# Expert rows loaded into all 128 partitions, the last weight chunks held, and three expert places of 32 tokens, in a hybrid SSD/GLA/MoE decoder step

## What is computed

```python
h2 = (rms_norm(x, p['norm2_w']) * (1 + sc2) + sh2).reshape(bt * s, D_MODEL)
comb = route(h2, w_router, router_bias)          # two experts of one group per token, weights sum to 1
for e in range(N_EXPERTS):
    ye = (jax.nn.silu(h @ wg[e]) * (h @ wu[e])) @ wd[e]
    out = out + comb[:, e:e + 1].astype(h.dtype) * ye
x = x + g2 * y_moe
```

## Time and profile before

| what | us |
|---|---|
| median of 3 runs | 1023.16 (1021.93 to 1028.83) |
| the profiled execution | 1020.22 |
| its span, first to last instruction | 1018.3 |

### The profile page before, as it was taken

The page is one execution under the profiler, slowest core; times in us unless marked ns, Lnnn a source line. Parts: engine busy times, 40 slices in busy tenths (PEclk is TensorE's granted clock), DMA queues, the critical chain, the costliest instruction groups (busy, mean ns, idle before and its releaser), DMA issues.

```text
span 1018.3 us, 18707 instructions
## 1 busy us (share of the span) xinstructions
PE 941.1 (92%) x7658; PEld 654.9 (64%) x7658; DVE 443.6 (44%) x1110; ACT 225.4 (22%) x459; POOL 151.4 (15%) x238
## 2 busy tenths in 40 slices
PE   5999999999999999999999999998999889889653
PEld 3667676676767566666666677665887658755331
DVE  3121234677347975666540711226534232232216
ACT  2240222323353322332251300003200011011012
POOL 0000232352021543233200000011100000000022
PEclk9999999999999999999999999999999989889996
DMA  9943345465455566546442633442899999999992
GB/s 375 393 151 124 125 165 189 168 232 176 170 189 206 206 221 212 207 168 238 164 150 88 254 122 125 188 184 89 291 354 388 374 382 383 364 390 375 364 383 79
DMA packets 47323, 239.43 MB, mean 235 GB/s; under 512 B 6896, under 2 KB 10576, under 8 KB 23920
## 3 DMA queue, kind: packets, MB, share of 16 engines
q1 hardware_dynamic: 42560, 227.74, 60.4%
q0 software_dynamic: 1552, 5.51, 1.6%
q10 hardware_dynamic: 3120, 4.92, 1.5%
HBM read 214.70 MB, written 23.83 MB: 234 GB/s over the span
## 4 chain that ended last, share of the span: by engine, by line
PE 73%; DMA 13%; SPq 6%; DVE 3%; issue 2%; ACT 1%; POOL 1%; POOLq 0%; ACTq 0%; DVEq 0%
PE pjB L939 16%; PE pjA L939 15%; PE pjA L1337 7%; PE pjB L1337 7%; DMA ring<-in_w 5%; SPq L869 5%; DMA regA<-xd 3%; DMA xsF<-xd 3%; PE states L1533 2%; PE states L1521 2%; PE states L948 2%; PE states L1524 1%; PE bank L1074 1%; PE states L1316 1%; PE states L1074 1%
## 5 line engine op out<-in xcount | busy, mean ns | idle before, releaser
L939 PE MATMUL pjA<-hF,ring 128*128 128x320 f32 x608 | 171.9, 436 | 0.5 <-ACT regA L1763 0.5
L939 PE MATMUL pjB<-hF,ring 128*128 128x320 f32 x608 | 171.8, 436 | 0.0
L939 PEld LDWEIGHTS pjA<-hF,ring 128*128 128x128 f32 x608 | 113.2, 190 | 50.6 <-issue 7.0
L939 PEld LDWEIGHTS pjB<-hF,ring 128*128 128x128 f32 x608 | 113.3, 190 | 48.6 <-issue 4.7
L1533 PE MATMUL states<-ring,oF 128*32 128x256 f32 x960 | 55.6, 380 | 7.6 <-DMA ring<-in_w 7.6
L2833 DVE STREAM_TRANSPOSE hF<-oF 32x64 f32<-32x64 f32 (+1 forms) x240 | 59.8, 249 | 3.1
L2816 DVE TENSOR_TENSOR oF<-oF,states 128x256 f32<-128x256 f32 (+1 forms) x16 | 7.5, 470 | 111.9 <-PE states L1533 59.3
L1533 PEld LDWEIGHTS states<-ring,oF 128*32 128x32 f32 x960 | 31.1, 110 | 30.4 <-DMA ring<-in_w 9.4
L2519 DVE TENSOR_TENSOR G<-G 128x320 f32<-128x320 f32 x32 | 48.8, 1564 | 0.0
L2122 POOL TENSOR_TENSOR G<-regA,G 128x128 f32<-128x128 f32 (+1 forms) x32 | 19.0, 595 | 192.3 <-ACT G L1819 192.3
L2221 POOL DMA_INDIRECT regA<-yd,idx x3 | 2.8, 938 | 267.7 <-DMA yd<-hF 267.1
(11 more groups left out here) (584 smaller groups left out, 1632.9 us busy)
## 6 DMA issues: line engine op xcount, KB each, us to landing
ring<-in_w SPq DMA_DIRECT2D x126, 1024.0 KB, 7.6
xsF<-in_w SPq DMA_DIRECT2D x14, 1024.0 KB, 29.4
regA<-in_w SPq DMA_DIRECT2D x13, 1024.0 KB, 28.8
rF<-in_w SPq DMA_DIRECT2D x8, 1024.0 KB, 29.4
bcF<-in_w SPq DMA_DIRECT2D x8, 1024.0 KB, 29.2
G<-in_ss SPq DMA_DIRECT2D x16, 512.0 KB, 4.2
out_ss_new<-G SPq DMA_DIRECT2D x16, 512.0 KB, 2.9
bp<-in_w SPq DMA_DIRECT2D x7, 1024.0 KB, 29.4
```

What stands on the lines that cost most here:

```text
L939: mm = pe.matmul(pj[g % 2][:, 0:T], w[:, k, half * P:half * P + P], hF[:, k, :], start=(k == 0), stop=(k == KT - 1))
```

## The change

Three things are done. **Row loads fill 128 partitions.** At a full place 128 rows are loaded (the last 32 are not used); at a small one the 64 rows are read as 128 half rows of 2 KB, partition 2r+h with half h of row r; at a tiny one 32 rows as 128 quarter rows of 1 KB. Four (or two) 128x128 transposes follow in place of eight, and the copies out of PSUM put halves and quarters in order. `xd` gets 128 spare rows in place of 96. **Three places of 32 tokens.** Places 5, 9 and 13 (`TINY_AT`) take the three emptiest experts but one; `tiled_tiny` gives each column group a quarter of the columns, 128, and the outputs go to `yd` in four stores of 32 rows x 1 KB. **Held last chunks.** Before the load of chunk (15, 2) SP waits until all even places, place 14 last, are stored in `yd`; chunks (15, 2) to (15, 5) follow it in SP's order. Besides, the residual add of tiles 0 and 1 moves from POOL to DVE, into `summed`.

Only changed lines stand here; a line of "..." marks what is left out between them.

```diff
@@ -154,15 +154,22 @@
+TINY_AT = (5, 9, 13)
...
-RANKED_AT = [p for p in FULL_AT if p not in FIXED_AT] + [p for p in range(E) if p not in FULL_AT]
+RANKED_AT = [p for p in FULL_AT if p not in FIXED_AT] + [p for p in range(LAST) if p not in FULL_AT + TINY_AT]
+RANKED_AT += list(TINY_AT) + [LAST]
...
-    return CAP if p in FULL_AT else SMALL
+    return CAP if p in FULL_AT else QUAD if p in TINY_AT else SMALL
...
+def width_of(p):
...
+    return WIDE if p in FULL_AT else P if p in TINY_AT else HALF
@@ -393,6 +400,8 @@
+        actQ = hF_[:, 4 * WIDE:6 * WIDE].rearrange("p (v x) -> p v x", v=2)[:, :, 0:4 * QUAD].rearrange(
+            "p v (k c) -> p v k c", k=4)
@@ -412,7 +421,7 @@
-        rowsB = [xsf[0:CAP, 0:D], regA[0:CAP, 2560 + CH:2560 + CH + D]]
+        rowsB = [xsf[:, 0:D], regA[:, 2560 + CH:2560 + CH + D]]
@@ -652,9 +661,29 @@
+        def stored(eng, v, n):
...
+            eng.wait_ge(s_yd[v], 16 * sum(4 if p in TINY_AT else 2 for p in range(v, LAST, 2)[:n]))
...
+        def turned_rows(p, part):
...
+            if p in FULL_AT:
+                return b[part][:, 0:4 * CAP].rearrange("p (k c) -> p k c", k=4)
+            if p in TINY_AT:
+                return b[part][:, 0:P].rearrange("p (r h) -> p h r", h=4)
+            return b[part][:, 0:2 * P].rearrange("p (k r h) -> p k h r", k=2, h=2)
...
+        def turned_to(p, part):
...
+            if p in FULL_AT:
+                return heF[:, p % 2, 4 * part:4 * part + 4, :]
+            if p in TINY_AT:
+                return heF[:, p % 2].rearrange("p (h k) c -> p k h c", h=4)[:, part, :, 0:QUAD]
+            return heF[:, p % 2].rearrange("p (h k) c -> p k h c", h=2)[:, 2 * part:2 * part + 2, :, 0:SMALL]
@@ -817,8 +846,8 @@
-            sp.dma_start(d["xd"][XROWS:XROWS + CAP, :],
-                         d["x"].rearrange("p k t -> (p k t)")[0:CAP * D].rearrange("(r c) -> r c", c=D)).then_inc(s_ld3, 16)
+            sp.dma_start(d["xd"][XROWS:XROWS + P, :],
+                         d["x"].rearrange("p k t -> (p k t)")[0:P * D].rearrange("(r c) -> r c", c=D)).then_inc(s_ld3, 16)
@@ -866,13 +895,20 @@
+                        if NEXT[m] == seq_of(LAST, 2):
+                            sp.wait_ge(s_yd[0], 32 * (E // 2))
...
-                sp.dma_start(rowsB[p % 2][0:cap_of(p), :], d["xd"][bass.ds(at, cap_of(p)), :]).then_inc(s_xe[p % 2], 16)
+                if p in FULL_AT:
+                    sp.dma_start(rowsB[p % 2], d["xd"][bass.ds(at, P), :]).then_inc(s_xe[p % 2], 16)
+                else:
+                    n = P // cap_of(p)
+                    sp.dma_start(rowsB[p % 2][:, 0:D // n],
+                                 d["xd"][bass.ds(at, cap_of(p)), :].rearrange("r (h c) -> (r h) c", h=n)).then_inc(s_xe[p % 2], 16)
@@ -1491,10 +1527,16 @@
-                n = cap_of(p)
-                for k in range(KT):
-                    mm = pe.transpose(b[k // 4][:, k % 4 * n:(k % 4 + 1) * n], rowsB[p % 2][0:n, k * P:(k + 1) * P],
-                                      ident[0:n, 0:n])
+                if p in FULL_AT:
+                    for k in range(KT):
+                        mm = pe.transpose(b[k // 4][:, k % 4 * CAP:(k % 4 + 1) * CAP], rowsB[p % 2][0:CAP, k * P:(k + 1) * P],
+                                          ident[0:CAP, 0:CAP])
+                elif p in TINY_AT:
+                    for k in range(2):
+                        mm = pe.transpose(b[k][:, 0:P], rowsB[p % 2][:, k * P:(k + 1) * P], ident)
+                else:
+                    for k in range(4):
+                        mm = pe.transpose(b[k // 2][:, k % 2 * P:k % 2 * P + P], rowsB[p % 2][:, k * P:(k + 1) * P], ident)
@@ -1534,9 +1576,17 @@
+            def tiled_tiny(bank, rows, w, first, last):
...
+                for q in range(4):
+                    at = QUAD * q
+                    mm = pe.matmul(bank[at:at + QUAD, 0:P], rows(0), w[:, P * q:P * q + P], start=first, stop=last,
+                                   tile_position=(0, at), skip_group_check=True)
+                return mm
...
-                he, full = heF[:, p % 2], p in FULL_AT
+                he, tiles = heF[:, p % 2], tiled if p in FULL_AT else tiled_tiny if p in TINY_AT else tiled_small
@@ -1549,15 +1599,14 @@
-                            mm = (tiled if full else tiled_small)(b[2 + part], rows, w[:, k, :], half + k == 0,
-                                                                  half == 1 and k == 3)
+                            mm = tiles(b[2 + part], rows, w[:, k, :], half + k == 0, half == 1 and k == 3)
...
-                act_ = (actT if full else actS)[:, p % 2]
+                act_ = (actT if full else actQ if p in TINY_AT else actS)[:, p % 2]
@@ -1567,8 +1616,8 @@
-                            mm = tiled_small(pj[h], lambda c: act_[:, k, QUAD * c:QUAD * c + QUAD], w[:, k, :],
-                                             k == 0, k == 3)
+                            tiles = tiled_tiny if p in TINY_AT else tiled_small
+                            mm = tiles(pj[h], lambda c: act_[:, k, QUAD * c:QUAD * c + QUAD], w[:, k, :], k == 0, k == 3)
@@ -1581,7 +1630,7 @@
-                pe.wait_ge(s_base if t == 2 else s_x3, 1 if t == 2 else t + 1)
+                pe.wait_ge(s_base, t + 1)
@@ -1992,13 +2041,11 @@
-                    n = cap_of(p)
-                    act.activation(heF[:, p % 2, 0:4, 0:n], b[0][:, 0:4 * n].rearrange("p (k c) -> p k c", k=4),
-                                   ACT.Copy).then_inc(s_hea, 1)
+                    act.activation(turned_to(p, 0), turned_rows(p, 0), ACT.Copy).then_inc(s_hea, 1)
...
-                    n = WIDE if p in FULL_AT else HALF
+                    n = width_of(p)
@@ -2007,10 +2054,10 @@
-                    n = BLOCKS if full else 2
+                    n = width_of(p) // P
...
-                        act.wait_ge(s_yd[v], 32 * (p // 2))
+                        stored(act, v, p // 2)
@@ -2020,6 +2067,10 @@
+                    elif p in TINY_AT:
+                        for h in range(4):
+                            act.dma_start(rows[:, 256 * h:256 * h + 256],
+                                          yE[QUAD * h:QUAD * h + QUAD, v, 0:256]).then_inc(s_yd[v], 16)
@@ -2062,7 +2113,7 @@
-                    act.wait_ge(s_base if t == 2 else s_x3, 1 if t == 2 else t + 1)
+                    act.wait_ge(s_base, t + 1)
@@ -2215,16 +2266,13 @@
-                    pool.wait_ge(s_yd[v], 32 * (E // 2 - v))
+                    stored(pool, v, E // 2 - v)
...
-                for t in range(2):
-                    pool.wait_ge(s_gm, t + 1)
-                    pool.tensor_tensor(hT[:, t, :], hT[:, t, :], xT[:, t, :], ALU.add).then_inc(s_x3, 1)
@@ -2793,22 +2841,20 @@
-                    n = cap_of(p)
-                    dve.tensor_copy(heF[:, p % 2, 4:8, 0:n], b[1][:, 0:4 * n].rearrange("p (k c) -> p k c", k=4)
-                                    ).then_inc(s_heb, 1)
+                    dve.tensor_copy(turned_to(p, 1), turned_rows(p, 1)).then_inc(s_heb, 1)
...
-                    v, n = p % 2, BLOCKS if p in FULL_AT else 2
+                    v, n = p % 2, width_of(p) // P
...
-                        dve.wait_ge(s_yd[v], 32 * (p // 2))
+                        stored(dve, v, p // 2)
...
-                    n = WIDE if p in FULL_AT else HALF
+                    n = width_of(p)
@@ -2827,6 +2873,8 @@
+                            elif p in TINY_AT:
+                                out, n = actQ[to, v, c:c + 1, :], P
@@ -2875,7 +2923,9 @@
-                    return gated(t, rows)
+                    cm(gated(t, rows))
+                    cm.wait()
+                    dve.tensor_tensor(hT[0:rows, t, :], hT[0:rows, t, :], xT[0:rows, t, :], ALU.add).then_inc(s_base, 1)
@@ -2885,13 +2935,11 @@
-                summed(0).then_inc(s_gm, 1)
+                summed(0)
...
-                summed(1).then_inc(s_gm, 1)
-                cm(summed(2))
-                cm.wait()
-                dve.tensor_tensor(hT[0:NSAMP, 2, :], hT[0:NSAMP, 2, :], xT[0:NSAMP, 2, :], ALU.add).then_inc(s_base, 1)
+                summed(1)
+                summed(2)
@@ -2996,7 +3044,7 @@
-        c[:, C_CP + p] = 0 if p in FULL_AT else CAP - SMALL
+        c[:, C_CP + p] = CAP - cap_of(p)
@@ -3085,7 +3133,7 @@
-    d["xd"] = nc.dram_tensor("xd", (XROWS + CAP, D), F32, kind="Internal").ap()
+    d["xd"] = nc.dram_tensor("xd", (XROWS + P, D), F32, kind="Internal").ap()
...

```

## The result

| kernel | median, us | runs | the profiled execution's span, us |
|---|---|---|---|
| before | 1024.0 (1021.93 to 1028.83) | 4 | 1018.3 |
| changed | 997.44 (995.32 to 1000.19) | 4 | 993.4 |

The ratio, time over that of the kernel before on the same chip, is 0.9736, with a 95% interval of 0.9689 to 0.9782: faster by 2.6%, some 27 us. The forecast was 999.5 us with a range of 989 to 1013.

What follows compares the result with a forecast made beforehand. The prediction took the DMA queue, slowed by narrow row loads, to bound the mixture. It summed 1020.2 - 23.5 + 0.5 = 997.2 us for an execution like the profiled one and forecast a median of 999.5 us, range 989 to 1013.

Steps and rivals of the forecast that it cites:

- What bounds the kernel: In the mixture, the DMA queue: it ends when its bytes have passed, at 375 GB/s where clean stretches reach about 420.
- Part 1, row loads: Up to the landing of place 15's rows, 128-partition loads gain 24.8 + 0.3 - 1.6 = 23.5 us; landing at 941.6.
- The 1.6 us kept back for small pieces and unevenness: In the mixture's row loads, a small cost assumed for 2 KB and 1 KB pieces and remaining unevenness: 1.6 us.
- Part 2, places of 32 tokens: At places 5, 9 and 13, TensorE's saving is worth nothing, as chunks load slower than they compute; only bytes count.
- Part 3, the hold: In the tail after place 15's rows land, the hold gives 3.4 us and contention takes about 4; taken as +0.5 us.
- first pair at about R+25.2, second at R+31.8: In the tail, gather landings in us after R, the landing of place 15's rows, with gathers getting a third beside chunks.
- The sum: For the whole kernel, 1020.2 - 23.5 + 0.5 = 997.2 us for an execution like the profiled one; median forecast 999.5 us.
- the signs named: From 734 on: 410 to 425 GB/s, chunks landing in 25 to 27 us, place 14's stores 4 to 5, gathers 14 to 17.
- Half the rate and no more: Rival, mixture: a 64-partition load's own bytes go at half rate, the only harm; 6.8 us in all, time 1016; chance 0.08.
- The source: Rival, mixture: dips come from reading scattered rows of `xd` from DRAM and stay; time 1022 to 1024; chance 0.05.
- TensorE: Rival: TensorE's lower clock eats its 23 us lead and another 9, or gathers wait; time 1008; chance 0.12 with the tail.
- The hold as a loss: Rival, tail: held chunks and last gather come late, end 4 to 5 us later, or 10; slower than before, chance 0.05.

Runs made afterwards that it cites:

- rows_only: The kernel before with only the change's row loads, turns and copies; no 32-token places, no hold, adds on POOL: 998.42 us, ratio 0.9761.
- front64: rows_only, but the 64-token places load 64 rows of 4 KB into partitions 0 to 63 in one transfer: 1017.5 us, ratio 0.9947.
- halves_apart: rows_only, but small places load 64 rows of 4 KB in two transfers, to partitions 0 to 31 and 64 to 95: 1008.79 us, ratio 0.9833.
- halves_stacked: rows_only, but small places load 64 rows of 4 KB in two transfers, to partitions 0 to 31 and 32 to 63: 1017.85 us, ratio 0.9913.
- two_transfers: rows_only, but small places load the 2 KB half rows in two transfers, to partitions 0 to 63 and 64 to 127: 1007.33 us, ratio 0.9848.

## Why the prediction was right, by its own steps

*What bounds the kernel.* Right. The mixture ended with its bytes, and their number at the clean rate was what it came to: from 734 to R 203.9 us at 420, 85.6 MB.

*Part 1, row loads.* The mechanism is shown by rows_only, front64 and the pair apart and stacked. The sum said R at 941.6, it was 937.9: 27.2 us for 23.5. Two terms were off. The 1.6 us kept back for small pieces and unevenness were nothing, at 420 with 1 KB and 2 KB pieces in it. And the loads of places 1 and 2 were counted at nothing because TensorE sets the pace there, but 728 to 734 moved 277 GB/s before and 413 in the changed kernel, 0.8 MB or 1.9 us more. Before and changed, each in a fence of its own:

```profile
728.00:734.00 6.00, 5.30 (x90) 4.70 (x87) 4.79 (x16) 0.49 (x1) 0.00 (x0) 1.00 0.96 277
```

```profile
728.00:734.00 6.00, 5.30 (x89) 4.70 (x82) 4.32 (x15) 0.49 (x1) 0.00 (x0) 1.00 1.03 413
```

The other profiles bear this out. In the six us from S+10 the seven kernels with wide loads move 389 to 424 GB/s, the six others 272 to 374.

*Part 2, places of 32 tokens.* "TensorE's saving is worth nothing" holds: it waits for the DMA before and after. Their bytes were put at 0.65 MB, 1.6 us; R-S of the six kernels with tiny places is 1.8 to 4.4 us below that of rows_only. The part above the bytes is no work of the tiny places. From S+16 on all of them run at 420, rows_only with 86.8 MB and the six with 84.9 to 86.0; ahead of that, where no tiny place's rows are loaded yet (the first, of place 5, are asked for at S+31 in the changed kernel), rows_only moves 299 GB/s and the six 310 to 373.

*Part 3, the hold.* The mechanism was right, a size was off. The step that missed is "first pair at about R+25.2, second at R+31.8". The stores landed sooner than put (first gather at R+14.0), but the pairs were weighed at R+27.5 and R+33.3, and the tail grew by 2.3 us for 0.5. The share in that step, a third for the gathers, was right. First the weighing of the first pair, then the DMA queues from 958 to 966 (packets, MB, share of the engines), q1 with the chunks and q0 with the gathers:

```profile
965.39 1.15 ACT L2083 ACTIVATE regA<-regA,G 128x1024 f32<-128x1024 f32 x1 [10.93 <-DMA xsF<-yd,idx]
```

```profile
q1 hardware_dynamic: 302, 2.20, 65.6%
q0 software_dynamic: 307, 1.13, 34.8%
```

What was put too short is the time until the gathers move at all. Their first bytes pass after 956, more than four us after the first issue at 951.92, while the chunks, issued at 951.38, move from 952 on; in the kernel before it was 2.5 us at most, from 983.49 to before 986. Why the start is later beside the chunks is open.

*The sum.* "The median minus most of the 23" is a slip: 1023.2 - 999.5 is 23.7, more than the 23.0 that the steps add up to. The two misses of 3.7 and 1.8 us have opposite signs, so that 999.5 is as close to 997.4 as it is partly by luck. Of the signs named, the rate and the sign of the gain came as said; chunks landed in 24.5 us, a little under 25 to 27, the stores of place 14 in 2.8 for 4 to 5, and the gathers took 19 to 20 us for 14 to 17.

*Rivals.* Half the rate and no more: out by front64, 1017.5 where it gives 1002. The Trainium skill's rule of the eight ports ("SBUF — State Buffer", "Door 1: The DMA port swizzle") names partitions 0 to 63 as one set of ports, and halves_apart and halves_stacked agree, 1008.8 against 1017.9. The loss by its port figures alone, an estimate of 0.6 us for a load, is too small: front64 shows 1.7. The source: out by rows_only and by two_transfers. TensorE: it had its lead throughout, and waited 2.6 us until 921.8 for the rows of place 14. The hold as a loss came true at 2.4 us by the profiles, far too little to turn the sign.

## What to carry to other kernels

When the DMA engines are busy all the time and yet move a rate that rises and falls, look at the rate in windows and at what lands in the slow ones: a small transfer to part of the partitions can cost everything queued beside it more than its own bytes take, here almost three times as much. Spread small loads over all 128 partitions in one transfer, by cutting rows into halves or quarters and putting them in order while they are turned, even where that loads rows that nobody uses. And a transfer held back to clear the way for another is not free where both end in the same wait: here what the stores won, the gathers lost.

## What was not expected of the hardware

A 64-partition load of 256 KB among the weight chunks costs 1.7 us where its bytes at the clean rate take 0.62, and the slow stretch is about ten us long (918 to 928 and 936 to 946 in the kernel before); the runs show no reason for its length. Stores from 64 partitions, and from 32, don't do that: in the changed kernel eight of 32 KB and ten of 128 KB are issued between 734 and R, a stretch that stays at 420 GB/s. And the same two half transfers are worth 9 us more or less by whether the second goes to partitions 32 to 63 or 64 to 95.
